# Streaming both parts of the activations through the upward feed-forward products

## What is computed

```python
def squared_relu_mlp(h, w_in, w_out):
    return jnp.square(jax.nn.relu(h @ w_in)) @ w_out

x = x + mix @ w_out[l]
x = x + squared_relu_mlp(rms_norm(x, norm_mlp_g[l]), w_mlp_in[l], w_mlp_out[l])
```

## Time and profile before

| | before |
|---|---|
| time of three runs | 1172.31, 1173.15, 1178.43 us, median 1173.15 |
| span of the profiled execution | 1178.0 us; its own total time isn't listed apart, the nearest run is 1178.43 |
| TensorE matmul busy | 1077.3 us, 91% |
| VectorE (DVE) busy | 780.7 us, 66% |
| ScalarE (ACT) busy | 580.5 us, 49% |
| GpSimd (POOL) busy | 184.5 us, 16% |
| mean granted TensorE clock | 0.915 of full speed |
| chain that ended last | PE 68%, DVE 21%, ACT 7%, issue 3% |

### The profile page before, as it was taken

The page is one execution under the profiler, slowest core; times in us unless marked ns, Lnnn a source line. Parts: engine busy times, 40 slices in busy tenths (PEclk is TensorE's granted clock), DMA queues, the critical chain, the costliest instruction groups (busy, mean ns, idle before and its releaser), DMA issues.

```text
span 1178.0 us, 18361 instructions
## 1 busy us (share of the span) xinstructions
PE 1077.3 (91%) x7222; PEld 976.0 (83%) x7222; DVE 780.7 (66%) x1507; ACT 580.5 (49%) x1062; POOL 184.5 (16%) x85
## 2 busy tenths in 40 slices
PE   5996699999999997898999999999889799999976
PEld 5995489899988996577998998896668699999865
DVE  4799785656678516576657656755744677777775
ACT  5542365444555324454554544545544466646454
POOL 1781011222121000000112212211000000000200
PEclk9996789999999955699999999997879899999988
DMA  8441024555454332000445455440121245454411
GB/s 338 176 148 71 1 107 152 188 186 192 170 194 172 112 124 91 1 1 36 179 144 214 171 188 190 169 152 36 37 108 72 108 145 182 178 212 166 175 54 36
DMA packets 22837, 158.33 MB, mean 134 GB/s; under 512 B 2528, under 2 KB 2784, under 8 KB 4448
## 3 DMA queue, kind: packets, MB, share of 16 engines
q1 hardware_dynamic: 21888, 153.51, 35.7%
q10 hardware_dynamic: 864, 3.65, 0.8%
HBM read 156.10 MB, written 1.05 MB: 133 GB/s over the span
## 4 chain that ended last, share of the span: by engine, by line
PE 68%; DVE 21%; ACT 7%; issue 3%; DMA 1%; POOL 0%; DVEq 0%; ACTq 0%
PE bank L666 64%; DVE obank L1750 5%; DVE split_lo L559 4%; ACT split_hi L551 2%; PE obank L666 2%; PE bank L796 1%; ACT hidden_parts L1240 1%; DVE square_sum L1742 1%; DVE hidden_parts L1742 1%; ACT L1240 1%; DVE mlp_lo L1750 1%; DVE x L1742 1%; DVE tmp L1750 1%; DMA consts<-in_consts 1%; ACT act_parts L1243 1%
## 5 line engine op out<-in xcount | busy, mean ns | idle before, releaser
L666 PE MATMUL bank<-act_parts,split_hi 128*128 128x256 f32 (+1 forms) x1632 | 332.1, 301 | 30.6 <-DVE split_lo L559 13.0
L559 DVE TENSOR_TENSOR split_lo<-ring,split_hi 128x1024 fp32r<-128x1024 f32 (+1 forms) x206 | 265.5, 1299 | 130.7 <-ACT split_hi L551 130.3
L551 ACT ACTIVATE split_hi<-ring 128x1024 fp32r<-128x1024 f32 (+1 forms) x280 | 287.8, 1045 | 114.1 <-PE bank L666 112.8
L559 POOL TENSOR_TENSOR split_lo<-ring,split_hi 128x1024 fp32r<-128x1024 f32 (+1 forms) x74 | 181.2, 2454 | 956.4 <-ACT split_hi L551 956.4
L666 PEld LDWEIGHTS bank<-act_parts,split_hi 128*128 128x128 f32 x1632 | 267.0, 198 | 41.8 <-issue 26.3
L666 PE MATMUL bank<-hidden_parts,split_hi 128*128 128x512 f32 (+1 forms) x816 | 265.5, 377 | 4.2 <-POOL split_lo L559 3.0
L666 PE MATMUL bank<-act_parts,split_lo 128*128 128x256 f32 x880 | 254.1, 289 | 0.0
L666 PE MATMUL bank<-hidden_parts,split_lo 128*128 128x256 f32 x752 | 210.2, 280 | 0.0
L666 PEld LDWEIGHTS bank<-hidden_parts,split_hi 128*128 128x128 f32 x816 | 148.7, 188 | 35.7 <-POOL split_lo L559 3.7
L666 PEld LDWEIGHTS bank<-act_parts,split_lo 128*128 128x128 f32 x880 | 174.8, 199 | 0.0
L666 PE MATMUL bank<-mlp_hi,split_hi 128*128 128x256 f32 x512 | 146.0, 285 | 4.9 <-DVE mlp_lo L1750 2.5
(11 more groups left out here) (226 smaller groups left out, 1309.2 us busy)
## 6 DMA issues: line engine op xcount, KB each, us to landing
ring<-in_weights SPq DMA_DIRECT2D x141, 1024.0 KB, 4.8
ring<-in_weights SPq DMA_DIRECT2D x5, 768.0 KB, 4.1
x<-in_x ACTq DMA_DIRECT2D x1, 1024.0 KB, 7.7
y<-in_mem ACTq DMA_DIRECT2D x1, 1024.0 KB, 9.7
out<-x SPq DMA_DIRECT2D x4, 256.0 KB, 2.5
consts<-in_consts ACTq DMA_DIRECT2D x1, 867.5 KB, 12.6
ring<-in_weights SPq DMA_DIRECT2D x1, 512.0 KB, 3.7
consts<-in_consts ACTq DMA_DIRECT2D x1, 260.0 KB, 7.7
```

Of the source, the lines that this page charges most:

```text
L551: nc.scalar.activation(split_hi[:, w % SPLIT, 0:n], src, ACT.Copy).then_inc(sem("high_parts"), 1)
L559: (nc.vector if engine == "vector" else nc.gpsimd).tensor_tensor(split_lo[:, w % SPLIT, 0:n], src, split_hi[:, w % SPLIT, 0:n].bitcast(F32 ...
L666: return nc.tensor.matmul(dst, lhsT, rhs, start=start, stop=stop)
```

## The change

The activations' high and low parts become one tensor mlp_parts, and the upward products of both blocks use linear_halves in place of linear. The low and high part of the activations' product now end in different halves of the bank. ACT copies the second half (columns 256 to 511) into slots2[t % 4], signalled by second_half; DVE adds the first half and that copy into slots[t % 4], which frees the bank, waits for its own result, and then does relu and scale from slots to slots, signalled by relu. ACT's squares wait for relu. The copy also waits until the low part of hidden tile t - 4 is made, since slots2 is used again. The third block's feed-forward part keeps linear.

```diff
-        with nc.sbuf_tensor("mlp_hi", [128, KD, SEQ], F32R) as mlp_hi, nc.sbuf_tensor("mlp_lo", [128, KD, SEQ], F32R) as mlp_lo:
-            pass
+        with nc.sbuf_tensor("mlp_parts", [128, 2, KD, SEQ], F32R) as mlp_parts:
+            mlp_hi, mlp_lo = (mlp_parts[:, part, :, :] for part in range(2))
...
-            def linear_halves(stage, first, count, parts):
+            def linear_halves(stage, first, count, parts, arriving=None):
...
                     for k in range(kts):
+                        if arriving is not None and t == first:
+                            pe.wait_ge(sem(arriving), k + 1)
                         last = half_products(dst, w, k, parts, k == 0, k == kts - 1)
...
                     elif n == 0:
-                        normed(name, into, act)
-                        linear(into, 3, sizes[0] * per - 3, act)
+                        linear_halves(into, 0, 2, act, f"{name}.act")
+                        folded_stat(name)
+                        linear_halves(into, 2, 1, act)
+                        full_bcast(name)
+                        linear_halves(into, 3, sizes[0] * per - 3, act)
+                    elif n < len(sizes) and per == 1:
+                        linear_halves(into, KD * n * per, sizes[n] * per, act)
                     elif n < len(sizes):
                         linear(into, KD * n * per, sizes[n] * per, act)
...
 (ACT)
-                            wait_emptied(act, into, t)
+                            if t >= 4:
+                                act.wait_ge(sem(f"mlp{l}.hidden"), t - 3)
+                            wait_tile(act, into, t)
+                            copy(slots2[:, t % 4, :], bank(into, t)[:, SEQ:2 * SEQ]).then_inc(sem(f"mlp{l}.second_half"), 1)
+                            act.wait_ge(sem(f"mlp{l}.relu"), t + 1)
                             do(slots2[:, t % 4, :], slots[:, t % 4, :], ACT.Square)
                             do(hidden_hi[:, n % 2, t % KD, :], slots[:, t % 4, :], ACT.Square).then_inc(sem(f"mlp{l}.high_hidden"), 1)
                             if t >= 2:
                                 pump(into, t)
...
 (DVE)
                             wait_tile(dve, into, t)
-                            stt(slots[:, t % 4, :], bank(into, t)[:, 0:SEQ], 0.0, rb[:, :], ALU.max, ALU.mult)\
-                                .then_inc(emptied(into, t), 1)
+                            dve.wait_ge(sem(f"mlp{l}.second_half"), t + 1)
+                            tt_(slots[:, t % 4, :], bank(into, t)[:, 0:SEQ], slots2[:, t % 4, :], ALU.add).then_inc(emptied(into, t), 1)
+                            wait_emptied(dve, into, t)
+                            stt(slots[:, t % 4, :], slots[:, t % 4, :], 0.0, rb[:, :], ALU.max, ALU.mult)\
+                                .then_inc(sem(f"mlp{l}.relu"), 1)
                             if t >= 2:
                                 pump(into, t)
```

More of the change, by code:

```diff
@@ L922, in _ @@
             projected = (act_hi, act_lo)
-            into_mlp = (mlp_hi, mlp_lo)
             def chunk_of(n):
@@ L1014, in mlp_block @@
             def mlp_block(l):
-                mlp(f"mlp{l}", f"mlp_in{l}", f"mlp_out{l}", f"mlp{l}.hidden", MLP_CHUNKS, 1, into_mlp)
+                mlp(f"mlp{l}", f"mlp_in{l}", f"mlp_out{l}", f"mlp{l}.hidden", MLP_CHUNKS, 1, mlp_parts)
             mlp_block(0)
```

## The result

The changed kernel takes 1240.38 us (median of 5 runs, 1230.37 to 1240.77) against 1178.43 us (median of 5, 1172.31 to 1179.44): ratio 1.0516, 95% interval 1.0473 to 1.056. It is 5% slower. The direction and the mechanism were forecast; the time lies 15 us above the forecast of 1225 and 4 above its range. The profiled execution, the fastest of the five, has a span of 1228.5 us against 1178.0; the other four took 1239 to 1241 us and left no trace.

The account below looks back on a forecast made before the run. The round through DVE and ACT was taken to bound the kernel. Its delays, 14.2 + 2 x 5.4 + 14.2 + 2 x 6.5, less 0.3 given back, made +51.9 us on 1173.15: 1225.1 us, range 1202 to 1236.

Parts of the forecast that it names:

- The bound: First 16 upward tiles of each feed-forward block: the 3.63 us round through DVE and ACT, not TensorE's 2.878, sets the pace.
- The unit costs: Per upward tile: DVE's extra add lengthens the round by 0.45 us; ACT's copy, 0.40, is free under split_lo.
- a pair: A POOL weight tile and its successor: 2.13 us later if the relu is held, 0.54 if not.
- the start of the chain: At a block's start three rounds run in series: first split_hi 3.31 us later, some 6.0 after rb.
- One sign: In each block's first 16 tiles, TensorE waits over 1 us before most tiles, for split_lo.
- The lock: Under POOL's split_lo, the relu with two SBUF inputs is held: some 2.0 us, ending 0.28 after POOL.
- the upper bound: Around a POOL weight tile, the relu is taken as held: +2.13 us, against +0.54 unheld.
- The clock: TensorE's granted clock might fall to 1.2 GHz in the first 32 tiles: +11 to +22 us, 15%, outside the sum.
- C: Rival: TensorE also loses clock in a quarter to half of the 32 first tiles, +11 to +22, about 1240 us; 15%.
- the forecast's own sign: In the two feed-forward blocks' stretches, granted clock below 1.00 would show the forecast wrong and the lost-clock rival right.
- A: The forecast case: longer round through DVE and ACT, relu held by POOL: 1225 us, own range 1216 to 1234; 55%.
- The base: Whole kernel before the change: median 1173.15 us, to which the unscaled delay of 51.9 was added.

Follow-up runs that it names:

- matmuls_only: Changed kernel with its new matmuls but without ACT's copy, DVE's add and the wait (one product left out): 1170.5 us, ratio 0.9958 to the kernel before.
- psum_relu: Changed kernel with DVE's sum written back to PSUM, so the relu has one SBUF operand: 1213.91 us, ratio 1.0331 to the kernel before.
- filler: Changed kernel with small unused bf16 products issued while TensorE waits for weights: 1232.28 us, ratio 1.048 to the kernel before.
- again: The changed kernel rerun unedited, for its spread and a second trace: 1234.75 us, ratio 1.0493 to the kernel before.

## Why the prediction was right and where it was wrong

**The bound.** Right. The round on DVE and ACT set the pace of the first 16 tiles, and matmuls_only shows how little the matmuls' new form can give while it does.

**The unit costs.** Right: the round grew by 0.47 (0.45 forecast), ACT's copy cost nothing where split_lo covers it, a pair that spans POOL's tile takes 8.51 us (8.5), the start of the chain puts the first split_hi 6.4 us after rb (6.0). Each block's first 16 tiles came out 14.6 us longer (14.2), the later eights of the first block at 295.24 - 258.26 = 36.98 against 275.2 - 243.77 = 31.4, +5.6 (5.4), those of the second at +6.6 (6.5).

```profile
258.26 0.40 PE L666 MATMUL bank<-mlp_parts,split_hi 128*128 128x512 f32 x1
...
295.24 0.79 PE L666 MATMUL bank<-hidden_parts,split_hi 128*128 128x512 f32 x1 [2.19 <-POOL split_lo L559]
...
310.84 0.39 PE L666 MATMUL bank<-mlp_parts,split_hi 128*128 128x512 f32 x1
```

One sign was stated too strongly: waits of over 1 us stand before five of the first 16 tiles in the first block and before six in the second, not before most.

**The lock.** Right, and shown by psum_relu: 17.2 us. The forecast took the upper bound, 2.13 a pair, on the form of one held instruction; the difference between its bounds was 19.

**The clock.** This is the step of the mechanism that failed: it stood in a rival of its own (C) and at nothing in the sum, as if it were one or the other. By the forecast's own sign, a granted clock below 1.00 in these stretches, part of C came true beside A. The waits that the sum itself produced are what lowers the clock, so a part of C belongs to A. Its price is 1.55 us after the first 16 tiles and 1.6 after the next eight (310.84 - 295.24 = 15.60 against 289.23 - 275.2 = 14.0), 3.1 us in the first block, of which filler wins back 3.0; rival C's 11 to 22 was far too much, since most of the low clock falls where TensorE waits anyway. With it and with 0.1 to 0.4 in each of the other terms the blocks cost 56.8 and not 51.9. C's remark that rows of half clock lie only in stages of small products overlooked rows of the kernel before; here a step of full-size products takes 0.64 us:

```profile
123.55 0.63 PE L666 MATMUL bank<-act_parts,split_hi 128*128 128x512 f32 x1
...
124.19 0.63 PE L666 MATMUL bank<-act_parts,split_hi 128*128 128x512 f32 x1
```

**The base.** This failed too, and costs about as much as the clock and the small terms together. I added the sum to 1173.15, the median of three runs, and wrote myself that the profiled execution was nearer to 1178.43; with more runs before stands at 1178.43, 1176.92 and 1177.48. Against 1177 the forecast would have been 1229, and 56.8 instead of 51.9 gives 1234: what `again` measured, 1234.75. The 15.3 us between 1225.1 and 1240.38 are so 5.3 of base, 3.1 of clock in the first block, 1.8 in the other terms of the blocks, and 5.1 outside them.

**What stays open.** In the first comparison the difference of the medians is 62 us, in the second 57.8, and the blocks account for 56.8 of either. The rest of the program, which no edit touches, moves by several us between executions. The runs show what this goes with: the changed kernel's run of 1230.37 us had a mean granted clock of 0.917 and its four of 1239 to 1241 one of 0.905 to 0.909; the kernel before took 1170.41 us at 0.924 and 1185.33 at 0.911. Why the clock differs between executions of the same code, no experiment shows, nor why it falls behind some waits of 2.2 us and not behind others.

## What to carry to other kernels

Before work is added to an engine that is half idle, follow one full round of waits through the engines: two engines at 49% and 66% were the bound here, since their instructions stood in one chain, and 0.45 us more in each round, with a DVE instruction held under POOL, cost more than the matmuls could give back. The remedy was not less work but another order: issue first what the others wait for and what itself waits for little (here the next weights' high part), and the same instructions take 2.27 us a round in place of 4.10. When a forecast makes a fast engine wait, its clock belongs in the sum; and when the runs' times spread by 0.5%, compare landmarks in the traces (here the rb copies), not spans.

## What the runs showed of the hardware

- In a TensorE that is otherwise busy, six of ten waits of 2.15 to 2.21 us are followed by a stretch at 1.2 GHz (0.51 in 209.90 to 213.30, 0.54 in 244.30 to 247.60); with small bf16 products in the waits the clock stays at 1.00. In psum_relu one such stretch follows a wait of 1.85 us.
- A DVE scalar_tensor_tensor with two SBUF operands that begins under a POOL tensor_tensor ends 0.28 us after it (1.87 us for 0.42); with the first operand in PSUM, also when it was just written there by DVE, it takes 0.42 (psum_relu).
- An add on DVE that writes back into the PSUM bank it reads takes 0.43 us, no more than one into SBUF (0.42).
- Executions of the same code differ in time with the mean granted clock: between the blocks 206.24 us at 0.83 and 215.35 at 0.78.
